# First token tile's work at each norm, the routing's order, and the mixers' order of taps, v and first inverse level

## What is computed

```python
for l in range(2):                       # attention layers
    u = x * (1 + scale) + shift          # scale, shift from c @ w_ada
    h = split_cols(u @ w_in)             # dsa, index, fox, nsa, gate columns
    y = (mix(h) * silu(h["gate"])) @ w_out
    x = layer_norm(ALPHA * x + (1 + gate) * y)            # norms 0, 1
for layer in range(2):                   # mixer layers
    h = x @ w_in                         # c_val, c_gate, q, k, v, z, b, a
    y_conv = silu(LN(causal_conv31(c_val * sigmoid(c_gate))))
    q, k, v = silu(causal_conv4([q, k, v]))
    y_dn = gated_delta_rule(q, k, v) * silu(z)            # needs (I + L)^-1 per head
    x = layer_norm(ALPHA * x + [y_conv, y_dn] @ w_out)    # norms 2, 4
    f = swiglu(x) if layer == 0 else moe(x)  # dense: 2816 wide; moe: 8 experts of 3584, top 2
    x = layer_norm(ALPHA * x + f)                         # norms 3, 5
```

## Time and profile before

| | |
|---|---|
| runs shown | 2247.93, 2742.0 and 3118.15 us; median 2742.0 |
| profiled execution | 2243.78 us, its span 2242.0 us |
| mean granted clock of TensorE | 0.951 |
| busy share of the span | PE 94%, DVE 67%, ACT 45%, POOL 2% |

### The profile page before, as it was taken

How to read it: one execution, slowest core, us unless ns; L and a number is a source line. 1 busy time by engine, 2 the same in 40 slices (tenths; PEclk the granted TensorE clock), 3 DMA queues, 4 the chain that set the end, 5 groups by cost and what they waited for, 6 DMA issues and landing times.

```text
span 2242.0 us, 27332 instructions
## 1 busy us (share of the span) xinstructions
PE 2115.7 (94%) x10276; PEld 1674.2 (75%) x10276; DVE 1506.6 (67%) x1824; ACT 999.3 (45%) x1063; POOL 53.5 (2%) x56
## 2 busy tenths in 40 slices
PE   7999989999998799989877999999999999999996
PEld 3785656765787499878755888888888888888885
DVE  4454423544279555436865988888888888889887
ACT  1111302112131244322223777767777777767674
POOL 0000000000002000000200000000000000000000
PEclk9998989889999899999887999999999999999999
DMA  9852033611520255453115999989999999989990
GB/s 344 283 189 81 29 122 113 217 38 38 173 95 19 68 176 188 169 186 137 38 38 189 369 361 339 374 327 371 331 368 348 350 346 353 372 324 374 326 373 19
DMA packets 238691, 502.15 MB, mean 224 GB/s; under 512 B 11258, under 2 KB 53010, under 8 KB 238610
## 3 DMA queue, kind: packets, MB, share of 16 engines
q1 hardware_dynamic: 238610, 501.03, 62.6%
HBM read 499.96 MB, written 1.05 MB: 223 GB/s over the span
## 4 chain that ended last, share of the span: by engine, by line
PE 90%; DVE 5%; issue 2%; ACT 2%; DMA 1%; SPq 0%; DVEq 0%; ACTq 0%
PE bank L1424 12%; PE bank L1407 9%; PE bank L1409 9%; PE bank L1408 9%; PE bank L760 7%; PE bank L1145 7%; PE bank L1121 4%; PE bank L1005 3%; PE bank L961 3%; PE bank L1309 3%; PE bank L1358 3%; PE bank L767 3%; PE bank L1100 2%; PE bank L1341 2%; PE bank L1343 2%
## 5 line engine op out<-in xcount | busy, mean ns | idle before, releaser
L2508 DVE TENSOR_TENSOR ring_r<-ring,his 128x2048 fp32r<-128x2048 f32 x240 | 548.8, 2290 | 84.9 <-ACT his L1517 84.9
L1517 ACT ACTIVATE his<-ring 128x2048 fp32r<-128x2048 f32 x240 | 460.1, 1918 | 136.0 <-PE bank L1409 78.9
L1407 PE MATMUL bank<-his,xe_hi 128*128 128x512 f32 x896 | 355.9, 397 | 1.7 <-DVE xe_lo L2516 1.4
L1409 PE MATMUL bank<-his,xe_lo 128*128 128x512 f32 x896 | 349.5, 390 | 0.0
L1408 PE MATMUL bank<-ring_r,xe_hi 128*128 128x512 f32 x704 | 274.1, 389 | 0.0
L2508 DVE TENSOR_TENSOR more_raw_r<-more_raw,his 128x2048 fp32r<-128x2048 f32 x96 | 219.8, 2291 | 32.1 <-ACT his L1517 32.1
L1517 ACT ACTIVATE his<-more_raw 128x2048 fp32r<-128x2048 f32 x96 | 184.2, 1919 | 57.4 <-PE bank L1424 31.9
L1407 PEld LDWEIGHTS bank<-his,xe_hi 128*128 128x128 f32 x896 | 168.3, 188 | 37.7 <-issue 1.7
L1409 PEld LDWEIGHTS bank<-his,xe_lo 128*128 128x128 f32 x896 | 168.1, 188 | 35.8
L760 PE MATMUL bank<-uT,ring 128*128 128x256 f32 (+3 forms) x640 | 152.2, 397 | 4.1 <-DVE uT L2015 2.7
L1408 PEld LDWEIGHTS bank<-ring_r,xe_hi 128*128 128x128 f32 x704 | 132.3, 188 | 28.3 <-issue 1.7
(11 more groups left out here) (418 smaller groups left out, 3067.8 us busy)
## 6 DMA issues: line engine op xcount, KB each, us to landing
ring<-in_moe_w_gate_dram SPq DMA_DIRECT2D x96, 1024.0 KB, 5.2
ring<-in_moe_w_up_dram SPq DMA_DIRECT2D x80, 1024.0 KB, 5.3
ring<-in_moe_w_down_dram SPq DMA_DIRECT2D x64, 1024.0 KB, 4.9
more_raw<-in_moe_w_down_dram SPq DMA_DIRECT2D x48, 1024.0 KB, 5.0
ring<-in_w_in_dram SPq DMA_DIRECT2D x16, 2048.0 KB, 8.6
more_raw<-in_moe_w_up_dram SPq DMA_DIRECT2D x32, 1024.0 KB, 5.3
ring<-in_w_ada_dram SPq DMA_DIRECT2D x12, 2048.0 KB, 8.9
ring<-in_w_out_dram SPq DMA_DIRECT2D x8, 2048.0 KB, 8.5
```

Of the source, the lines that this page charges most:

```text
L1407: mm(bank[b][:, :], xe_hi[:, k, :], hi[:, kk, :], start=(k == 0), stop=False)
L1409: last = mm(bank[b][:, :], xe_lo[:, k, :], hi[:, kk, :], start=False, stop=(k == KD - 1))
L1517: return go(out, in_, ACT.Copy, scale=scale)
L2508: tt(piece_lo(s), piece_raw(s), piece_hi(s).bitcast(fp32), ALU.subtract).then_inc(S("lo_ready"), 1)
```

## The change

No arithmetic is added or removed. These things change:

1. **Turning by tile.** `turn_tile(key, norms, i)` turns one token tile into two banks (`xT{i}0`, `xT{i}1`, four feature blocks each). For tile 0 it stands ahead of the last output product of the stage before; its banks are copied by ACT while that product runs. Then PE does the next stage's first projections on tile 0 alone, turns tile 1, and does the same projections on tile 1. This holds for norms 0 to 3; for norm 4 tile 0 goes through the router first. Layer 0's first turn stays as it was.
2. **End of a mixer.** `mix_out(i, c, half)` is called per half of the columns, starts after `cb0` alone, and is interleaved with the turns of the delta half.
3. **Dense layer.** ACT and DVE split the first two weight slots before mixer 0's residual instead of after it (ACT after its copies of `yd`). The first slot's gate and up products run per tile (128 moving columns), the others as before. `z3` and some banks move so that nothing overlaps.
4. **Middle of a mixer.** DVE: 5 taps ahead of `ss` instead of 2, 1 tap more ahead of `short(4)`, first level of `X` right after `Lw`, `attn` after it, `XT` after that; `short(5)` at level 1 in place of its taps, `vb` at level 2, 3 taps at level 6, and the last tap after `o0`. PE: `LT` ahead of `project("v", 1, 1)`, `vt` at level 2, z in other gaps. ACT: `to_pad(5)` after the `LT` copies, `silu(5)` after level 1's `Y`.
5. **Routing.** Logits per tile in two banks. ACT splits pieces 0 and 1 before the gates' exponential; DVE does its part of piece 0 between the tiles' logits and of piece 1 after `pick`. `pick` comes as soon as places are there (`first_pick`); `pickc` and gates are combined between the two halves of the gathered rest; the item list is made between the two first chunks, and the loop count is read after them. The first chunk starts on half of the gathered features.

```diff
+            def turn_tile(key, norms, i):
+                pe.wait_ge(S("x_ready"), NT * (norms - 1) + i + 1)
+                for half in range(2):
+                    j = jobs[(*key, f"xT{i}{half}")]
+                    b = take(pe, j)
+                    for kk in range(4):
+                        k = 4 * half + kk
+                        last = nc.tensor.transpose(b[:, kk * P:(kk + 1) * P], x[:, i, k * P:(k + 1) * P], C("ident"))
+                    done(last, j)
...
+                    turned((l,), 0)
+                    b = take(pe, j)
+                    feat(b, l, "idx_q", 0, P, 0, first)
+                    feat(b, l, "idx_q", P, P, T, first)
+                    b2 = take(pe, j2)
+                    feat(b2, l, "dsa_q", 0, P, 0, first)
+                    turn_tile((l,), l, 1)
+                    feat(b2, l, "dsa_q", P, P, T, first)
+                    turned((l,), 1)
...
                     for c in range(2):
+                        if (i, c) == (NT - 1, 1):
+                            turn_tile((l + 1,) if l + 1 < DEPTH else ("mix", 0), l + 1, 0)
                         j = jobs[l, f"wo{i}{c}"]
...
-                for name in ("c_gate", "c_val"):
-                    for half in range(2):
-                        project(name, half, 0)
-                        project(name, half, 1)
+                turned(("mix", m), 0)
+                for half, f in ((0, 0), (0, 1), (1, 0)):
+                    project("c_gate", half, f, tile(0))
+                turn_tile(("mix", m), q, 1)
+                project("c_gate", 1, 1, tile(0))
+                turned(("mix", m), 1)
...
+                copied(pe, J("cb0"))
+                mix_out(0, 0, 0)
+                mix_out(0, 1, 0)
                 for i in range(NT):
                     pe.wait_ge(S("delta_ready"), NT * m + i + 1)
                     j = J(f"yd{i}")
                     done(transposes4(take(pe, j), lambda h: o[:, i, hs_(h)]), j)
+                copied(pe, J("cb1"))
+                mix_out(1, 0, 0)
+                copied(pe, J("yd0"))
+                mix_out(0, 0, 1)
+                mix_out(0, 1, 1)
+                mix_out(1, 1, 0)
+                copied(pe, J("yd1"))
+                mix_out(1, 0, 1)
+                turn_tile(after, q + 1, 0)
+                mix_out(1, 1, 1)
...
+                turned(("ffn", 0), 0)
+                gate_up(0, 0, 0, first)
+                gate_up(0, 0, 1, first)
+                gate_up(0, 1, 0, first)
+                turn_tile(("ffn", 0), DEPTH + 1, 1)
+                gate_up(0, 1, 1, first)
+                turned(("ffn", 0), 1)
...
                     for n in range(NDOWN - 2, NDOWN):
+                        if (i, n) == (NT - 1, NDOWN - 1):
+                            turn_tile(("mix", 1), DEPTH + 2, 0)
                         down(n, [i])
...
+                if m == 0:
+                    split_ff(0)
+                    split_ff(1)
+                for i in range(NT):
+                    residual(("mix", m), "wo", i, 0, z2[:, i, :])
+                    if i and m == 0:
+                        low_tile(0)
+                    residual(("mix", m), "wo", i, 1, z2[:, i, :])
+                    norm(q, i, z2[:, i, :])
...
-                taps(2)
+                taps(5)
                 j = J("ss")
...
+                taps(1)
                 short(4)
...
-                taps(CONV_WIN - taken[0])
                 j = J("o0")
                 b = filled(dve, j)
                 free(tt(by_head(o[:, 0, :]), ...), j)
+                taps(CONV_WIN - taken[0])
                 j = J("o1")
...
+                gathered_lo(0, [0])
+                combine()
+                gathered_lo(0, [1])
+                chunk(0, -2)
+                list_items()
+                chunk(0, -1)
+                dve.wait_ge(S("items_ready"), 1)
```

More of the change, by code:

```diff
@@ L333, in add @@
         jobs.add(("moe", 0, name), bank, frees)
-    for n in range(4):
-        add(f"xT{n}", n)
-    add("logits", 4); add("places", 5)
+    for n, b in enumerate((3, 7, 4, 6)):
+        add(f"xT{n // 2}{n % 2}", b)
+    add("logits0", 2); add("logits1", 1); add("places", 0)
 LAST_USE.update({"k": "k23", "q": "q23", "v": "v23", "c_gate": "c_gate23", "c_val": "c_val23", "z": "z1",
@@ L1101, in _ @@
                         done(last, j)
[L1103 to L1110, removed]
-                                                       x[:, i, (2 * m + kk) * P:(2 * m + kk + 1) * P], C("ident"))
-                        if i == NT - 1:
-                            done(last, jobs[(*key, f"xT{m}")])
-                if wait_copies:
-                    for m in range(4):
-                        copied(pe, jobs[(*key, f"xT{m}")])
             def heads4(b, lhsT, rhs):
@@ L1709, in mixer @@
                         free(copy(Y[:, i, :], filled(act, j)[:, :]), j)
+                    if s == 1:
+                        silu(5)
                 z_silu(1)
@@ L2335, in mixer @@
                     free(last, j)
-                for i in range(NT):
-                    j = J(f"at{i}")
-                    b = filled(dve, j)
-                    free(tt(attn[:, i, :], b[:, :], decay[:, i, :], ALU.mult), j)
-                short(5)
                 lv = CONST_AT["levels"][0]
@@ L2464, in experts @@
                 tt(gates[:, :, 0], best[:, :, 1], best[:, :, 0], ALU.subtract).then_inc(S("gap_ready"), 1)
+                dve.wait_ge(S("chosen_ready"), 1)
+                link(ts(places[:, :, 0:NE], chosen[:, :, :], FAR, -FAR, ALU.mult, ALU.add))
                 dve.wait_ge(S("gap_exp"), 1)
@@ L2478, in experts @@
                 link(tt(places[:, :, 0:NE], places[:, :, 0:NE], b[:, 0:NT * NE].rearrange("p (i e) -> p i e", i=NT), ALU.add))
-                link(ts(places[:, :, NE:], places[:, :, 0:NE], -float(P), None, ALU.add))
+                for i in range(NT):
+                    last = ts(pick[:, i, :], C("iota"), places[:, i, 0:1], None, ALU.is_equal)
+                last.then_inc(S("first_pick"), 1)
                 dve.wait_ge(S("silu_table"), 1)
                 free(nc.vector.tensor_copy(long[:, 0, :], b[:, NT * NE:NT * NE + NE]), j)
-                copied(dve, j)
@@ new lines, in combine @@
+                def combine():
+                    for i in range(NT):
+                        link(ts(comb[:, i, 0:NE], hot[:, 0, i, :], gates[:, i, 2:3], None, ALU.mult))
+                        link(stt(comb[:, i, 0:NE], hot[:, 1, i, :], gates[:, i, 3:4], comb[:, i, 0:NE], ALU.mult, ALU.add))
+                    link(nc.vector.tensor_copy(comb[:, :, NE:], comb[:, :, 0:NE]))
+                    for i in range(NT):
+                        last = ts(pickc[:, i, :], C("iota"), places[:, i, 0:1], comb[:, i, 0:1], ALU.is_equal, ALU.mult)
+                    last.then_inc(S("picked"), 1)
```

465 lines of the change are left out of this document (260 added, 205 removed).

## The result

The changed kernel takes **2195.0 us** (median of 4 runs, 2193.1 to 2196.0). Against the kernel before, 2248 us, that is a ratio of **0.976, 95% interval 0.974 to 0.979**: 2.4%, some 53 us. The 2742 shown with the kernel before is the middle of one fast and two slow runs (2247.9, 2742 and 3118, with a fourth of 2248.1), and only fast runs are compared here. On the profiled executions the span fell from 2242.0 to 2191.0. The forecast was 2174, with a range of its own from 2162 to 2188. The direction was right, but the time lies 7 us above that range: the forecast expected 70 us less on the profile, and 51 came.

What follows compares the result with a forecast made beforehand. PE bounds the kernel, so time is gained only where it stands or runs at half clock. Gains 9.4 + 8.4 + 6.6 + 7.7 + 29.2 + 8.4 = 69.7 from 2243.8 give 2174 us, range 2162 to 2188.

Steps and rivals of the forecast that it cites:

- norm 2's term: Mixer end and dense layer's first slot, split by tile: gain 6.6 us; 9 at price 0.067, -1 at 0.12.
- the mixers' term: Middle of the mixers, waits for DVE and half clock removed: gain 14.6 us per mixer, 29.2 for both, bounds 8 and 18.
- norms 0, 1, 3: PE's work on tile 0 covers the wait for tile 1's x: gains 9.4, 8.4 and 7.7 us.
- I take 0.08, the narrow row with its start taken off.: Dense layer's first slot: an fp32r product of 128 columns costs 0.08 us, bounds 0.067 and 0.12.
- over 20 us for the 192 narrow products: Dense layer's first slot: the forecast is wrong if these take over 20 us; 15.4 was expected.
- Levels 2 to 6 are PE's own 5.3 us each plus z, and stay so.: Mixers' levels: PE alone sets their pace, putting `vn0` at 718.4 instead of 726.9.
- level 1 for `short(5)`: Mixers' levels: level 1 now waits for `short(5)`, listed under time given back, with no size of its own.
- the way to the first level product: Mixers' middle: reordered DVE and PE work brings that product to 671.1 instead of 676.8.
- the end of the mixers: From `vn0`: fewer last taps and no 5.84 us wait at the last delta product, with half clock 6.1 us more gained.
- the routing: Norm 4 and routing: first expert product 9.4 us earlier after the first output product, gain taken as 8.4.
- rival 2: DVE limits the mixers, taps slowed beside POOL: 17 us less gained there, 5 less in routing, 2196 us; chance 0.17.
- Rival 3: Dense layer's first slot: narrow fp32r products cost what fp32 costs, 27 us more, 2201 us; chance 0.05.

Runs made afterwards that it cites:

- x5_no_cover: Changed kernel with tile 1's turn ahead of all projections at norms 0, 1 and 3, tile 0 still turned early: 2217.1 us, ratio 0.986.
- x13_short_quarter: `x1_z_moved` with three of four taps of the short convolution left out for v's last pair of rows: 2185.8 us, ratio 0.972.
- the repeat: The changed kernel run once more, unaltered, as common base for the runs beside it: 2195.3 us, ratio 0.977.
- x1_z_moved: Changed kernel with the z projection's parts one step later, none after level 2: 2188.6 us, ratio 0.974.
- x9_z_tail: `x1_z_moved` with z's last two parts put behind the turn of the convolution and one tap moved from level 6 behind it: 2182.9 us, ratio 0.971.

## Why the prediction was wrong, and where it was right

Two terms of the sum failed: the price of the narrow fp32r product in norm 2's term, and the levels in the mixers' term. The range failed with them. It says 2162 to 2188 from norm 2 at -1 to 9 and the mixers at 8 to 18 each, but these bounds add up to 2165 to 2195: 7.6 and twice 6.6 above 2174. Both terms came out near their lower bounds, and the time with them.

**Right: what bounds the kernel, and norms 0, 1, 3.** PE's waits at the norms and the half clock behind them were the place to look. Norm 0 gained 8.6 to 9.8 up to its first projection (forecast 9.4, with the half clock behind it), norm 1 gained 8.5 (8.4), norm 3 gained 7.7 (7.7). `x5_no_cover` shows the mechanism named: taking PE's work on tile 0 away gives the time back, at norm 0 to within 0.4 us, at norms 1 and 3 and 1 us more. The covers' timing held as well (at norm 2 x of tile 0 at 28.2 us behind the first output product, the last one ending at 32.8).

**Wrong: "I take 0.08, the narrow row with its start taken off."** The price is 0.112. At 0.08 the split slot costs 15.4 us, it costs 21.5: 6.1 of the 18.7 missing. The prediction had named over 20 us for the 192 narrow products as a sign of being wrong. With 0.112 its own sum gives 0.5 for norm 2; counted as there, with the 1.4 for `cb0`, the stage shows 0.7 and 1.7. The row at 174.20 to 174.56 showed 0.12 for the narrow product as it stood. The correction came from another row, a product of 256 columns behind a wait, and nothing showed that the narrow ones had started as late: at 0.112 three of them take 0.34 of their 0.36. The fp32 instruction of 128 columns, 0.111, was a stream and the nearest row.

**Wrong: "Levels 2 to 6 are PE's own 5.3 us each plus z, and stay so."** The levels took 51.2 and 52.8 where the prediction puts 47.3 (671.1 to 718.4). They take 47.39 once two waits are gone (`x13_short_quarter`). What the step left out is the bank. z's part 0 was put between v's turn and level 3, and it writes the bank from which DVE still has to read that turn, behind its taps and sums. The table of banks stood in the code; moving a consumer means asking who still holds its buffer. With the half clock that follows in some profiles this is 1.7 to 3.4 per mixer. Level 1's wait, 2.05 with what hangs on it, was seen ("level 1 for `short(5)`") but not taken off the levels' sum.

**Nearly right: the way to the first level product** (4.6 for 5.7) **and the end of the mixers** (6.6 for 7.5, with the 1.4 for `cb0`). The mixers' term was 14.6 each, bounded by 8 and 18. Without the 1.4 for `cb0` the changed kernel shows 8.7 and, in the repeat, 7.1; alone on the kernel before the new middle shows 10.4.

**Right in sum, one part open: the routing.** 7.3 to 9.1 for 7.0. Of the item list, counted as 2 us out of the way, 1.1 to 2.9 shows in a profile, and the time can't confirm it.

**The rivals.** The time, 2195, is beside rival 2's 2196, but its mechanism is not what happened. It had DVE as the limit, with the taps slowed by POOL; `x1_z_moved`, `x9_z_tail` and `x13_short_quarter` each took a wait or a piece of PE's work out of the levels, and the levels became shorter by all of it. With z moved DVE stalls PE in the levels by more than 1 us in one place, level 1, where 8 instructions of `short(5)` take 5.4 us beside POOL's masks. What filled rival 2's number is the bank and the price. Rival 3 gave the narrow fp32r product fp32's price, two instructions of 0.111; fp32r takes one, and costs what one costs.

**Left open.** What the item list's place is worth. And why the clock falls behind the same wait in one execution and not in the next: the 1.7 us that the experts' stage took longer in the first profile are of that kind (last section).

## What to carry to other kernels

Splitting a product by tile to start earlier is free only while the engine's price follows the columns. Take it from a stream of the same width and type, and if the row as it stands and a corrected one differ, go by the row as it stands. When work is moved into a gap, look up which buffer it writes and who still has to read it. And price a wait with the clock behind it: 3.9 us of useless products in a wait of 4.3 us gained 6 us in all. Real work moved into the same wait (z's last parts) pays for the place it leaves; that it pays for the clock too is not shown.

## What the runs showed of the hardware

**A floor per product.** Thirty-two fp32 instructions with one moving column, at full clock, in the repeat of the changed kernel (PE timeline, then windows):
```profile
637.21 3.63 PE L1235 MATMUL bank<-const,sq 128*128 128x1 f32 x32
640.70 5.39 PE L1162 MATMUL bank<-uT,ring 128*128 128x256 f32 x16
```
```profile
639.00:640.00 1.00, 1.00 (x11) 1.00 0.00 0
640.00:641.00 1.00, 1.00 (x9) 1.00 0.06 16
641.00:642.00 1.00, 1.00 (x5) 0.65 0.00 0
642.00:644.00 2.00, 2.00 (x6) 0.50 0.00 0
```
3.49 us for 32 is 0.109 each, as much as with 128 columns. The Trainium skill (TensorE: Matmul & The Clock Gate, section LDWEIGHTS) puts the loading of weights at their columns / 1.2 ns, 107 ns for 128. An estimate from it is that a product with weights of its own costs 107 ns at least, however narrow; the rows at 1 and at 128 columns agree. The same page (Back-to-back issue gap) gives about 81 ns for a sustained stream of such pairs at 128 columns; the fp32r stream here shows 112, and the measurement decides.

**The clock fell with PE busy.** In those windows PE never stands, and yet the clock falls to 0.50 at 641.3, right behind the one-column products; the 16 instructions that follow take 5.2 us for 3.5. In the first profile it fell at 632.3, while they were still running (629.6 to 633.9). So this stretch of one-column products was followed by half clock, as waits were.

**Steps of 1.65 us.** Stages with the same code and the same waits come at two lengths: 64.9 or 66.6 to the first level product, 51.2 or 52.8 in the levels, 998.7 or 1000.4 in the experts. In each of them the longer one has 3.4 us more at half clock: 10.2 against 6.8 on the way to the first level product, 3.4 against none in the other two. Windows over the levels and over the experts' end, in the first profile:
```profile
654.00:705.00 51.00, 46.29 (x312) 1.00 0.13 41
2165.00:2170.00 5.00, 5.00 (x16) 0.67 0.00 0
```
and in the repeat:
```profile
660.00:713.00 53.00, 48.33 (x314) 0.97 0.12 40
2171.00:2176.00 5.00, 5.00 (x23) 1.00 0.00 0
```
Both profiles have the wait of 2.65 us in the levels, and both have one of 1.93 us in front of the experts' last products. In the repeat the clock fell behind the first of these waits alone, in the first profile behind the second alone. A difference of 1.65 us between two single profiles says nothing about the kernels.
